# Points between VectorE's long runs at which weight halves and stream matmuls can be issued, in two recurrences of a fused transformer kernel

## What is computed

```python
u = rms_norm(h) * norm_pre_mix
p = u @ w_in                                  # 2048 x 7952
o_ret  = retention(p[:, 0:2048])              # chunked linear attention with decay
o_hgrn = hgrn2(p[:, 2048:4096], lower_bound)  # gated linear recurrence
o_ml   = mlstm(p[:, 4096:6160])
o_rw   = rwkv7(p[:, 6160:7952])               # state recurrence with a rank-one correction
h = h + rms_norm(concat(o_ret, o_hgrn, o_ml, o_rw) @ w_out) * norm_post_mix
u = rms_norm(h)
h = h + rms_norm((silu(u @ w_gate) * (u @ w_up)) @ w_down) * norm_post_ffn   # inner width 5632
```

## Time and profile before

| | |
|---|---|
| Median of 3 runs | 3939.21 us (3934.56 to 3942.47) |
| The profiled execution's own time | 3938.35 us |
| Its span in the profile | 3937.0 us |
| PE busy | 3795.7 us (96%) |
| PE weight loads busy | 3213.3 us (82%) |
| VectorE busy | 2259.9 us (57%) |
| ScalarE busy | 1792.9 us (46%) |
| HBM read | 623.04 MB |

### The profile page before, as it was taken

The page is one execution under the profiler, slowest core; times in us unless marked ns, Lnnn a source line. Parts: engine busy times, 40 slices in busy tenths (PEclk is TensorE's granted clock), DMA queues, the critical chain, the costliest instruction groups (busy, mean ns, idle before and its releaser), DMA issues.

```text
span 3937.0 us, 49183 instructions
## 1 busy us (share of the span) xinstructions
PE 3795.7 (96%) x19948; PEld 3213.3 (82%) x19948; DVE 2259.9 (57%) x3526; ACT 1792.9 (46%) x2517; POOL 106.8 (3%) x61
## 2 busy tenths in 40 slices
PE   6999999999999999989999999999999999999998
PEld 5886778787898998778888888888888778888887
DVE  4565666766566746665445444566646664444444
ACT  5454455545454424444444444554325454444443
POOL 0000000000010000000000000010000000000000
...
GB/s 191 191 160 163 150 114 172 167 189 115 166 179 147 125 23 149 134 150 188 191 189 187 202 193 193 173 133 150 62 50 157 151 157 189 190 189 190 200 193 170
DMA packets 342050, 628.34 MB, mean 160 GB/s; under 512 B 21712, under 2 KB 64672, under 8 KB 340800
## 3 DMA queue, kind: packets, MB, share of 16 engines
...
HBM read 623.04 MB, written 2.10 MB: 159 GB/s over the span
## 4 chain that ended last, share of the span: by engine, by line
PE 89%; DVE 5%; ACT 3%; POOL 1%; issue 1%; ACTq 1%; DMA 0%; DVEq 0%; POOLq 0%
PE bank L603 74%; DVE weights_low L511 2%; PE bank L727 2%; PE bank L1242 1%; PE bank L1339 1%; PE bank L2440 1%; PE bank L2454 1%; PE bank L2047 1%; PE bank L2453 1%; PE bank L582 1%; ACT weights_high L498 1%; PE bank L1322 1%; POOL stat L688 1%; PE bank L1245 0%; ACTq L753 0%
## 5 line engine op out<-in xcount | busy, mean ns | idle before, releaser
L511 DVE TENSOR_TENSOR weights_low<-weights,weights_high 128x1024 fp32r<-128x1024 f32 (+3 forms) x1176 | 1398.3, 1199 | 985.1 <-ACT weights_high L498 974.2
L498 ACT ACTIVATE weights_high<-weights 128x1024 fp32r<-128x1024 f32 (+3 forms) x1176 | 1205.0, 1029 | 1338.7 <-PE bank L603 1284.4
L603 PE MATMUL bank<-weights_high,x_high 128*128 128x512 f32 (+3 forms) x2816 | 1114.2, 396 | 26.4 <-DVE weights_low L511 11.6
L603 PE MATMUL bank<-weights_high,x_low 128*128 128x512 f32 (+3 forms) x2816 | 1087.5, 386 | 0.0
L603 PE MATMUL bank<-weights_low,x_high 128*128 128x512 f32 (+3 forms) x2816 | 1087.2, 386 | 0.0
L603 PEld LDWEIGHTS bank<-weights_high,x_high 128*128 128x128 f32 x2816 | 536.7, 191 | 137.0 <-DVE weights_low L511 23.5
L603 PEld LDWEIGHTS bank<-weights_low,x_high 128*128 128x128 f32 x2816 | 536.5, 191 | 101.8
L603 PEld LDWEIGHTS bank<-weights_high,x_low 128*128 128x128 f32 x2816 | 537.4, 191 | 93.2
L603 PE MATMUL bank<-x_high,weights_high 128*128 128x256 f32 x960 | 279.9, 292 | 10.8 <-DVE arena L632 4.7
L603 PE MATMUL bank<-x_low,weights_high 128*128 128x256 f32 x960 | 274.2, 286 | 0.0
L603 PE MATMUL bank<-weights_high,ff_high 128*128 128x512 f32 x704 | 274.0, 389 | 0.0
(11 more groups left out here) (380 smaller groups left out, 3618.3 us busy)
## 6 DMA issues: line engine op xcount, KB each, us to landing
...
weights<-in_w_ffn_gate_dram SPq DMA_DIRECT2D x176, 512.0 KB, 3.7
weights<-in_w_ffn_up_dram SPq DMA_DIRECT2D x176, 512.0 KB, 3.6
weights<-in_w_ffn_down_dram SPq DMA_DIRECT2D x176, 512.0 KB, 3.6
weights<-in_w_out_dram SPq DMA_DIRECT2D x128, 512.0 KB, 3.7
...
```

The costliest lines, as they stand in the source:

```text
L498: self.high_mark[g] = self.high_split.count(act.ran(nc.scalar.activation(high, raw, ACT.Copy)), act.clock)
L511: self.low_mark[g] = self.low_split.count(dve.ran(nc.vector.tensor_tensor(low, raw, high.bitcast(F32), ALU.subtract)), dve.clock)
L603: ins = pe.ran(nc.tensor.matmul(out, l, r, start=(u + c + x + y == 0), stop=(u == blk.n - 1 and c == UNIT - 1 and y == 1)))
```

## The change

It adds `yield` at 21 places of `hgrn`, `rwkv` and the helpers `cumulate`, `scale` and `merge`, which become generators where they weren't; the reciprocal of 128x1024 becomes four of 128x256 with a `yield` after each. `cumulate` gives such a point after every second scan, `merge` after every masked copy. No other instruction is added or taken away. The diff:

```diff
--- before.py
+++ after.py
@@ -1837,6 +1837,8 @@
         one = self.c("ones")[:, 0:1].broadcast_to([P, width])
         for k in range(0, src.shape[1], width):
             dve.did(nc.vector.tensor_tensor_scan(out[:, k:k + width], one, src[:, k:k + width], 0.0, ALU.mult, ALU.add))
+            if k // width % 2:
+                yield
         dve.wait_ge(dve.now())
 
     def head_rms_gate(self, y, z, gain, tmp):
@@ -1991,19 +1993,22 @@
         else:
             qd, kd = mixed
             dve.did(nc.vector.tensor_scalar(qd, f, 0.0, None, ALU.min))
+            yield
             act.wait_ge(dve.did(nc.vector.tensor_scalar(kd, f, 0.0, None, ALU.max)))
             dve.did(nc.vector.tensor_tensor(v3(k), v3(k), over(keep), ALU.mult))
             yield
             act.did(nc.scalar.activation(qd, qd, ACT.Exp))
             dve.wait_ge(act.did(nc.scalar.activation(kd, kd, ACT.Exp, scale=-1.0)))
             dve.seq(nc.vector.tensor_tensor(v3(kd), v3(kd), over(lb), ALU.mult))
+            yield
             dve.seq(nc.vector.tensor_tensor(qd, qd, kd, ALU.add))
+            yield
             act.wait_ge(dve.seq(nc.vector.tensor_scalar(qd, qd, 2.0 ** -60, None, ALU.max)))
             yield
             dve.wait_ge(act.did(nc.scalar.activation(qd, qd, ACT.Ln)))
             dve.seq(nc.vector.tensor_tensor(f, qd, E0, ALU.subtract))
         yield
-        self.cumulate(cum, f, P)
+        yield from self.cumulate(cum, f, P)
         yield
         pool.wait_ge(dve.now())
         act.wait_ge(dve.now())
@@ -2055,16 +2061,16 @@
                 dve.wait_ge(multiplied[lev, g])
                 self.bank_free[4 + g] = [dve.did(nc.vector.copy_predicated(
                     acc[g].rearrange("p (i s) -> p i s", i=4), m, self.ps[4 + g][:, :].rearrange("p (i s) -> p i s", i=4)))]
+                yield
 
         exponents(0)
         yield from multiply(-1, k, q)
         yield
         exponents(1)
-        merge(-1, self.c("ident"))
-        yield
+        yield from merge(-1, self.c("ident"))
         dve.wait_ge(landed)
         for lev in range(LEVELS):
-            scale(lev)
+            yield from scale(lev)
             yield
             if lev + 2 < LEVELS:
                 exponents(lev + 2)
@@ -2073,7 +2079,7 @@
             yield from multiply(lev, mixed[lev % 2], mixed[lev % 2])
             yield
             dve.wait_ge(dve.now())
-            merge(lev, masks[:, lev, 1, :])
+            yield from merge(lev, masks[:, lev, 1, :])
         c3, E3, d3 = v3(cum), v3(E0), v3(mixed[1])
         dve.wait_ge(multiplied[5, 3], act.now(), dve.now())
         dve.did(nc.vector.tensor_tensor(E3[:, :, 0:P], c3[:, :, P - 1:P].broadcast_to([P, 4, P]), c3[:, :, 0:P], ALU.subtract))
@@ -2294,7 +2300,7 @@
         yield wanted
         pe.wait_ge(*wanted)
         dve.wait_ge(m)
-        self.cumulate(L_, lw, P)
+        yield from self.cumulate(L_, lw, P)
         yield
         yield
         for g in range(2):
@@ -2307,16 +2313,22 @@
         for c in range(4):
             dve.did(nc.vector.tensor_scalar(shifted[:, c * S:(c + 1) * S], c4(a)[:, c, :], 1.0, par("rwkv_k_a_2", c), ALU.subtract, ALU.mult))
         dve.wait_ge(dve.now())
+        yield
         dve.seq(nc.vector.scalar_tensor_tensor(k, shifted, 1.0, k, ALU.add, ALU.mult))
         yield
         for c in range(4):
             m2 = dve.did(nc.vector.scalar_tensor_tensor(eP[:, c * S:(c + 1) * S], c4(r)[:, c, :], par("rwkv_r_k_2", c), c4(k)[:, c, :],
                                                         ALU.mult, ALU.mult))
+        yield
         dve.wait_ge(m)
         dve.seq(nc.vector.tensor_scalar(sq, sq, 1e-12, None, ALU.max))
-        dve.seq(nc.vector.reciprocal(sq, sq))
-        yield
+        yield
+        for c in range(4):
+            dve.did(nc.vector.reciprocal(sq[:, c * S:(c + 1) * S], sq[:, c * S:(c + 1) * S]))
+            yield
+        dve.wait_ge(dve.now())
         dve.seq(nc.vector.tensor_tensor(kk, kk, sq, ALU.mult))
+        yield
         dve.did(nc.vector.tensor_tensor(a, a, kk, ALU.mult))
         yield [m2, *self.bank_free[4]]
         pe.wait_ge(m2, *self.bank_free[4])
```

## The result

| | before | changed |
|---|---|---|
| Median | 3938.64 us (12 runs, 3933.88 to 3943.90) | 3949.84 us (12 runs, 3942.04 to 3953.80) |
| Ratio | | 1.0024, 95% interval 1.0016 to 1.0031 |
| Span of the profiled execution | 3937.0 us | 3949.5 us |

The changed kernel is slower by 0.24% by the ratio (the two medians are 11.2 us, 0.28%, apart), where 3936 us and no measurable difference were forecast. The time is just inside the stated range; its side is that of the second rival.

What follows compares the result with a forecast made beforehand. PE was taken as the bound, busy 96%, so only its idle time and clock could give: gains −23.0, costs +3.4, +9.5, +4.9 and +2.0, sum −3.2 us, 3936 us against 3939.2; range 3921 to 3950.

Steps and rivals of the forecast that it cites:

- second rival: Bare retention end costs more in both layers, 13.5 us each: +9.4 us in sum, 3948.5 us, chance 0.20.
- The stalls in the recurrences: PE's waits at VectorE runs without a yield shrink: −10.8 us in layer 1, −5.4 us in layer 0.
- The clock behind these stalls: Four stalls of 2.8 us or longer each cost about 1.7 us of PE clock, won back: −6.8 us.
- the rest of the 0.94: Long stretch's clock, 0.94 over 380 us, loses 23 us; stalls explain some 5, the remainder was left unplaced.
- Cost one: Between mlstm's last matmul and the retention's transposes, VectorE bounds: PE idles 8.0 us in layer 1, +3.4; layer 0, 0.
- Cost two: Retention's normalisation and turn lose their covering stream matmuls at its end: +9.5 us in layer 1, +4.9 in layer 0.
- Cost three: Turns of hgrn's and rwkv's outputs come earlier, among mlstm's small matmuls: 1.0 us in each layer, +2.0 us.
- Its sign: Profile sign of the second rival: stalls of 10 us or more at the retention's end in both layers.
- Its point: The second rival decides when fewer than 65 matmuls are left behind the last head; both layers are below.
- first rival: It pays off: low halves in stock ahead of the retention, short end costs no clock; −14 us, 3925 us, chance 0.30.

Runs made afterwards that it cites:

- gap3: The change, but the planner holds back the last 3 pieces (9 stream matmuls) until the retention's 16 transposes are issued; 3943.01 us, ratio 1.0006.
- split_only: The kernel before with only the reciprocal split in four and a yield after each quarter; 3933.98 us, ratio 0.9987.
- unsplit: The change with the reciprocal in one piece again, one yield behind it; 3929.61 us, ratio 0.9971.
- u28: unsplit with the last 28 pieces (three stream matmuls each) held back until the retention's rotations are issued; 3930.53 us, ratio 0.9973.
- u40: unsplit with the last 40 pieces (three stream matmuls each) held back until the retention's rotations are issued; 3922.68 us, ratio 0.9956.

## Why the prediction was wrong

**The stalls in the recurrences** were forecast to fall by 10.8 us in layer 1, and fell by (16.13 − 8.45) + 3.68 = 11.4: right as a sum, not in its parts, since hgrn's place got a new stall of 4.33 us (a low half beside GpSimd) in exchange. In layer 0 5.4 was forecast and 3.36 + 0.1 measured. The half that I took of the 5.95 us there was not to be had.

**The clock behind these stalls** (5.1 us in layer 1) did not come. The lost clock of the recurrences is 23.8 us where it was 23.7. The 1.7 us behind the stall of 3.68 did come back, but a stretch at 0.50 from 2704 to 2714, behind a wait of 1.16 us that was there before too, took more. The prediction left open where the rest of the 0.94 falls: 17 of the 23.7 us lie where PE doesn't wait at all.

**Cost one, the stage ahead of the retention,** was right as idle time. 8.0 us of idle PE were forecast between mlstm's last matmul and the transposes, and the row of 3088.7 to 3135.7 has 47.0 − 38.9 = 8.1. It came in another form, 5.82 us of it as one stall at the turn of mlstm's output, and the clock behind that stall, 2.8 us, has no term in the sum. VectorE was busy for 38.6 of the 47 us, 82%, where over 85% was foretold.

**Cost two, the bare end,** was right as idle time: 8.3 + 1.35 forecast in layer 1, 8.29 + 1.57 measured, and 5.8 + 1.35 against 5.13 + 1.57 in layer 0. The 2.76 and 1.16 us at the old turns of layer 1 went.

**Cost three** was forecast at 1.0 in a layer; PE idles for 61 − 58.37 = 2.6 us over 3040 to 3101.

**The step that failed** is the clock in the sum, and most of it in cost two, where it says that PE "then runs at the lower clock, 3.8 us": the price of the clock at the end of layer 1 was counted behind the end's stall alone. It fell at the start of the heads, about 1 us behind two waits under 1 us each, and PE had 0.50 over all the other heads. From the second pair of L1918 to the end the heads took 3140.24 to 3160.28, 20.0 us, against 3105.05 to 3116.42, 11.4, before: +8.7 us. From 3040 to the norm the lost clock grew by 13.2 us where 3.8 were forecast: some 9.5 in the heads, 2.8 behind the 5.82 us stall, 2.6 behind the end, less the 1.7 that was lost there before. That is 9.4 us of the miss, and the 5.1 of clock that didn't come back ahead are the next. Idle time adds 3: the two waits (1.6) and cost three (1.6). The miss itself is 15 us, as −2.0 was forecast for layer 1 and +13.0 measured; these terms are some 2 to 3 us more, since lost clock is an estimate. gap3, which fills the two waits and has a longer one ahead of them, is 7 us below the change.

**The rivals.** The second gave the side and the time (3948.5), but not the mechanism, and its nearness is luck: it charged both layers' ends and took the clock from the normalisation's stall. Its sign, stalls of 10 us or more in both layers, is missing in layer 0, with 6.7. In fact layer 0, with 14 pieces, came out even (its norm starts 0.2 us earlier), and split_only and unsplit show that a layer with 14 pieces is no loss as a whole. Its point, 65 matmuls, was too high for that: with 39 behind the last head the layer is already even, and what decides is whether the first pieces reach the seam ahead of the heads. The first rival, with its sentence from the Trainium skill ("Perfetto Trace Analysis", Optimizing Scalar/DVE Operations), had a chance of 0.30. At the reciprocal it held (4.11 us became 0.72); over the kernel it didn't, since the new points changed what was issued some 370 us later.

**Not settled.** Why the same split leaves 14 pieces in one kernel and 0 in the other can be read from the order and not from the hardware: it comes of the planner's estimated clocks, and which estimate tips it was not tried. Nor was it tried which of rwkv's other points bring the unsplit kernel's 10 us, nor what brings the clock down where PE doesn't wait. u28, expected between unsplit and u40, isn't.
